# A fused two-block transformer kernel: memory keys interleaved with the mixing projection, and rotation by quarter-partition writes

## The chip, the cores and the metric

The kernel runs on one core of one Trainium2 chip. The metric is the device time of one launch in microseconds; lower is better. All matrix work here is float32, and TensorE (PE in the rows) is kept supplied by ScalarE (ACT), VectorE (DVE) and one DMA queue whose instructions SyncE (SPq) issues. GpSimd does next to nothing.

## The reference, cut to what matters

The reference is a transformer block with latent attention, memory cross-attention and a 16-expert layer, followed by a second block with gated linear attention. Only the first block holds the changed work:

```python
q_rope = apply_rope(q[..., QK_NOPE:], cos, sin)      # per head pair: 2 heads x 64 columns, 512 tokens
k_rope = apply_rope(kr, cos, sin)
y_mla  = mla_attention(q_nope, q_rope, k_nope, k_rope, v) @ w_mla_out
x = x + (g_conv * y_conv + g_mla * y_mla) @ w_mix_out            # the mixing projection
q = rmsnorm(x, norm_mem_g) @ w_mem_q                             # the memory norm feeds only q
k, v = split(rmsnorm(mem, norm_memkv_g) @ w_mem_kv)              # 256 memory rows, no need of x
# apply_rope: v1, v2 = halves of 32; out = [v1*cos - v2*sin, v1*sin + v2*cos]
```

Sizes: model width 1024 (8 tiles of 128), 512 tokens, 256 memory rows, 8 attention heads taken in 4 pairs, rotary width 64.

## The kernel before, in words

Activations lie transposed: model columns on the 128 partitions, tokens along the row. Every large product is made from three passes of float32r matmuls: each operand is split into a rounded high part and the rest, and `mm3` (L636 to L638) issues high by high, low by high and high by low. So a weight has to go through a small pipeline before TensorE may use it:

- SyncE loads a **unit** of 8 x 256 columns (1 MB) into one of two `raw` slots, once the unit two before it has been split (`w_lo_ready`).
- ScalarE makes the high part (`split_hi`, L1606), once TensorE has finished the unit two before it, whose slot it overwrites.
- VectorE makes the low part (`split_lo`, through `rest`, L2156), and TensorE may begin.

The order of units is the list `STREAM`, and all engines walk it in their own hand-written program order; each engine is strictly in order, and semaphores join them. A unit gives two output tiles of 128 columns. `dense_tiles` walks them with 24 matmuls each and cycles through four PSUM banks (`tile`), waiting until the earlier result in the bank has been consumed.

**The memory stage.** Four units of the mixing projection (`mix_out`, 512 tokens wide) come first; VectorE adds each result to `X`. Then come four units of memory keys (`mk`) and four of memory values (`mv`), each 256 columns wide, and after them four units of memory queries (`mq`), whose right-hand side is the normalised `X` in `H_hi` and `H_lo`. Their results of keys and values are split again by ScalarE (L1787) and VectorE (`mk_lo`, `mv_lo`). The norm of `X` runs inside the key and value units: squares (L1618), their sums, a matmul with ones (`norm_sums`, after `mk` unit 1), the root, a reciprocal (L2176), and then eight tiles, each made by VectorE into `T` (L2179), rounded by ScalarE (`his`, L1628) and its rest taken by VectorE (`h_lo`). `T` has two buffers. Which tiles follow which unit is the table `MEM_NORM_AT`. On ScalarE a unit is: copy of tile 0, `split_hi(u + 2)`, copy of tile 1, `his`. On VectorE it is: `split_lo(u + 2)`, the two rests, `norm_split`. The first tile of `mq` waits for `h_lo_ready` in front of each of its eight k steps, one norm tile more at each.

**The rotation.** For each head pair t the 128 rotary query rows `("qrope", t)` come out of TensorE. ScalarE copies them to `qr`; TensorE multiplies by a signed permutation `rot_c` (`rotate`, L741); VectorE (`rope`, L2282 to L2286) forms PSUM * sin + qr * cos, casts and takes the rest. Inside the pair loop the PE order behind the last transposes of a pair is `project_key(t+1, 0)`, `rotate`, `values(t, 3)`, `project_head(t+1, 1)`, then a wait for `queries(t+1, 0)` (`qk_lo_ready` 4t+5), `project_key(t+1, 1)`, a wait for `keys(t+1, 0)` (4t+6), two `project_value`, two `fill` and the scores of the next pair. VectorE runs `turned(t, 3)`, `queries`, `keys`, `rotated`. The same happens once to the keys' rotary rows `kr` (L708), in the first convolution unit.

**The experts** follow: their weights are streamed by SyncE into buffers that come free as TensorE finishes with them.

Of the kernel before, what the change touches and what calls it, by code (L numbers as in the profile page):

```python
# [63 lines left out]
for _name, _n in VEC_SIZES:  # L64
# [5 lines left out]
N_ROPE = 4  # L70
# [3 lines left out]
STREAM = [("lat", 2), ("conv", 12), ("conv_out", 4), ("glog", 8), ("mla_out", 4), ("mix_out", 4),  # L74
          ("memkv", 8), ("memq", 4), ("mem_out", 4), ("zk", 1), ("zlr", 1),
# [7 lines left out]

EUNITS = 12
MEM_NORM_AT = {2: (0, 1), 3: (2,), 4: (3, 4), 5: (5,), 6: (6, 7)}
# [69 lines left out]
def build(nc, t, out):  # L155
    with ExitStack() as ctx:
# [24 lines left out]
        rot_at = at[0]  # L181
        rot_c = fixed("rot_c", [P, P])
        tri = place("tri", [P, P], F32, rot_at)
# [56 lines left out]
        qr = place("qr", [P, S], F32, R + 113 * K)  # L240
# [141 lines left out]
        meta_sq_ready = sem("meta_sq_ready")  # L382
        meta_std_ready = sem("meta_std_ready")
        meta_n_ready = sem("meta_n_ready")
        meta_hi_ready = sem("meta_hi_ready")
        meta_lo_ready = sem("meta_lo_ready")
# [17 lines left out]
        qr_copied = sem("qr_copied")  # L404
# [208 lines left out]
        def _(pe):  # L613
# [60 lines left out]
            pe.wait_ge(meta_sq_ready, 1)  # L674
# [18 lines left out]
            for i in range(4):  # L693
                u = U0["conv"] + 3 * i
                dense_tiles(u, "xc", 2 * i, S, H, lambda m: (xc_copied, m + 1), ready=(h_lo_ready, 0))
                if i == 0:

                    pe.wait_ge(std_ready, 1)
                    pe.wait_ge(lat_sq_ready, 2)
                    for k in range(2):  # L700
                        ins = pe.matmul(bank[4][:, :], ones[:, :], sq[:, k, :], start=(k == 0), stop=(k == 1))
                    mark(ins, "ss_q")
                    pe.wait_ge(lat_sq_ready, 3)
                    pe.wait_ge(meta_std_ready, 1)
# [33 lines left out]
            def rotate(t, b):  # L738
                pe.wait_ge(qr_copied, t + 1)
                marks.tile = b  # L740
                mark(pe.matmul(b[:, :], rot_c[:, :], qr[:, :], start=True, stop=True), ("rot_q", t))  # L741

# [8 lines left out]
            for i in range(4):  # L751
                if i == 3:
# [4 lines left out]
                    rotate(0, bank[7])  # L757
                    w = unit(U0["conv_out"] + 3)
                    for j in range(2):
                        if j == 1:  # L760
                            project_head(0, 1, bank[4])
# [5 lines left out]
                            project_value(0, 1, bank[7])  # L767
# [73 lines left out]
            for t in range(PAIRS):  # L841
# [54 lines left out]
            for i in range(4):  # L896
                dense_tiles(U0["mix_out"] + i, "mix_out", 2 * i, S, H, lambda m: (x_ready, m + 1),
                            ready=(m_lo_ready, 0))

            M = [MM_hi, MM_lo]  # L900
            for i in range(4):
                dense_tiles(U0["memkv"] + i, "mk", 2 * i, MEM, M, lambda m: (mkv_ready, m + 1),
                            ready=(mem_lo_ready, 0))
                if i == 1:
                    norm_sums("mem")

            for i in range(4):
                u = U0["memkv"] + 4 + i
# [7 lines left out]
                marks.at[("unit", u)] = marks.at[("mv", i, 1)]  # L916
            for i in range(4):
# [680 lines left out]
        def _(act):  # L1598
# [32 lines left out]
            act.activation(meta_sq[:, :, :], meta[:, :, :], ACT.Square).then_inc(meta_sq_ready, 1)  # L1631
            for m in range(KT):
# [9 lines left out]
                if m == 2:  # L1642
                    done(act, "meta_ss")
                    act.activation(meta_sq[:, 0, :], bank[5][:, 0:META], ACT.Sqrt, bias=eps, scale=1.0 / D)\
                       .then_inc(meta_std_ready, 1)
# [6 lines left out]
            act.wait_ge(meta_n_ready, 1)  # L1652
            act.activation(meta_hi[:, :, :], meta[:, :, :], ACT.Copy).then_inc(meta_hi_ready, 1)
# [32 lines left out]
            for i in range(4):  # L1686
                if i == 3:
                    copy(("qrope", 0), qr[:, :], qr_copied)
# [28 lines left out]
            for t in range(PAIRS):  # L1717
# [15 lines left out]
                if more:  # L1733
                    copy(("qrope", t + 1), qr[:, :], qr_copied)
                    copy(("q", t + 1, 0), qn_hi[:, 0, :], qk_hi_ready)
# [35 lines left out]
            for i in range(4):  # L1771
                for k in (2 * i, 2 * i + 1):
                    act.wait_ge(mem_n_ready, k + 1)
                    act.activation(MM_hi[:, k, :], memx[:, k, :], ACT.Copy).then_inc(mem_hi_ready, 1)
                split_hi(U0["mix_out"] + i + 2)
            squares("mem")
            for i in range(8):
                for j in range(2):
                    if i < 4:
                        o = done(act, ("mk", 2 * i + j))  # L1780
                        dst = mk_hi[:, 2 * i + j, :]
                    else:
                        o = done(act, ("mv", i - 4, j))
                        dst = mv_hi[:, j, (i - 4) * UC:(i - 3) * UC]
                    if j:
                        split_hi(U0["memkv"] + i + 2)
                    act.activation(dst, o[:, 0:UC], ACT.Copy).then_inc(mkv_hi_ready, 1)  # L1787
                if i == 1:
                    root("mem")
                if i in MEM_NORM_AT:  # L1790
                    his("mem", MEM_NORM_AT[i])
# [124 lines left out]
            act.wait_ge(meta_lo_ready, 1)  # L1916
# [228 lines left out]
        def _(dve):  # L2145
# [72 lines left out]
            def latent(m, dst):  # L2218
# [8 lines left out]
            dve.wait_ge(meta_std_ready, 1)  # L2227
# [6 lines left out]
               .then_inc(meta_n_ready, 1)  # L2234
            dve.wait_ge(meta_hi_ready, 1)
            rest(meta_lo[:, :, :], meta[:, :, :], meta_hi[:, :, :]).then_inc(meta_lo_ready, 1)
# [43 lines left out]
            def rope(src, dst, o, s, hi, lo):  # L2280

                link(dve.tensor_tensor(out=T[:, 0, :], in0=o[:, :], in1=sin_t[:, :], op=ALU.mult))  # L2282
                link(dve.tensor_tensor(out=T[:, 1, :], in0=src, in1=cos_t[:, :], op=ALU.mult))
                link(dve.tensor_tensor(out=dst, in0=T[:, 0, :], in1=T[:, 1, :], op=ALU.add))
                link(dve.tensor_copy(hi, dst))
                rest(lo, dst, hi).then_inc(s, 1)  # L2286

            done(dve, "rot_k")
            dve.wait_ge(c_lo_ready, KT)
            dve.wait_ge(rope_in, 16 * N_ROPE)  # L2290
            rope(kr[:, :], kr[:, :], bank[6], lat_ready, kr_hi[:, :], kr_lo[:, :])
# [18 lines left out]
            def rotated(t):  # L2310
                o = done(dve, ("rot_q", t))
                rope(qr[:, :], qr[:, :], o, qrr_ready, qr_hi[:, :], qr_lo[:, :])

            for i in range(4):
                if i == 3:
                    queries(0, 0)
                    keys(0, 0)
                    rotated(0)
# [37 lines left out]
            for t in range(PAIRS):  # L2356
# [47 lines left out]
            for i in range(4):  # L2404
                for k in (2 * i, 2 * i + 1):
                    dve.wait_ge(mem_hi_ready, k + 1)
                    rest(MM_lo[:, k, :], memx[:, k, :], MM_hi[:, k, :]).then_inc(mem_lo_ready, 1)
                for m in (2 * i, 2 * i + 1):
                    o = done(dve, ("mix_out", m))
                    dve.tensor_tensor(out=X[:, m, :], in0=o[:, :], in1=X[:, m, :], op=ALU.add).then_inc(x_ready, 1)  # L2410
                split_lo(U0["mix_out"] + i + 2)
            accumulate("mem")
            dve.wait_ge(x_ready, KT)
            for i in range(8):
                split_lo(U0["memkv"] + i + 2)
# [854 lines left out]
```

## Time and profile before

| | |
|---|---|
| device time, three runs | 1876.14, 1876.35, 1881.18 us; median 1876.35 us |
| span of the profiled execution (first to last instruction) | 1877.1 us |
| the profiled execution's own time | not listed apart from the three runs |
| busy: PE, PE weight loads, DVE, ACT | 1831.2, 1365.5, 1007.7, 631.1 us |
| mean granted TensorE clock | 0.993 |
| HBM traffic | 321.25 MB read, 172 GB/s over the span |

A row of a timeline reads: start us, duration us, engine, line, operation, output <- inputs, shapes, count of merged instructions, and in brackets how long the engine had been idle before and what ended that. Back-to-back instructions overlap a little, so the distance between starts is what one of them costs its engine. Granted clock 1.00 is 2.4 GHz, 0.50 is 1.2 GHz.

### The profile page before, as it was taken

How to read it: one execution, taken by the hardware profiler on the slowest of the kernel's cores; microseconds unless marked ns; L12 is line 12 of the kernel's file. 1: busy time of each engine (PE TensorE's matmuls, PEld its weight loads, DVE VectorE, ACT ScalarE, POOL GpSimd, SP SyncE). 2: the span in 40 equal slices, each digit the busy share in tenths (PEclk: the TensorE clock that was granted, in tenths of full speed). 3: DMA queues.
4: the chain of work that ended last, by engine and by line, in shares of the span. 5: the costliest groups of instructions: out<-in, count | busy, mean ns of one | idle time of the engine just before them, and what ended most of it. 6: DMA issues, size and time to landing. Idle time of an engine off the chain costs nothing.

```text
span 1877.1 us, 23248 instructions
## 1 busy us (share of the span) xinstructions
PE 1831.2 (98%) x9860; PEld 1365.5 (73%) x9860; DVE 1007.7 (54%) x1472; ACT 631.1 (34%) x921; POOL 0.2 (0%) x4
## 2 busy tenths in 40 slices
PE   7999999999999999999999999999999999999998
PEld 6788777788887886343443443797888779988998
DVE  6654366633565643222212322756766799777775
ACT  5322245433243421211112111444442345343331
POOL 0000000000000000000000000000000000000000
PEclk9999999999999999999999999999999999999999
DMA  6223211032244327999999999323221223323231
GB/s 188 90 90 94 86 51 37 24 116 90 90 135 135 109 116 314 428 427 427 429 427 427 427 428 417 116 75 90 83 74 46 90 68 113 112 91 110 92 113 46
DMA packets 136007, 324.85 MB, mean 173 GB/s; under 512 B 7504, under 2 KB 118368, under 8 KB 122464
## 3 DMA queue, kind: packets, MB, share of 16 engines
q1 hardware_dynamic: 135760, 322.32, 46.2%
q8 instruction: 78, 1.28, 0.3%
q10 hardware_dynamic: 144, 1.05, 0.1%
q14 instruction: 25, 0.20, 0.0%
HBM read 321.25 MB, written 2.10 MB: 172 GB/s over the span
## 4 chain that ended last, share of the span: by engine, by line
PE 83%; DMA 8%; DVE 5%; ACT 2%; issue 1%; SPq 0%; DVEq 0%; ACTq 0%
PE bank L636 20%; PE bank L637 19%; PE bank L638 19%; PE bank L1124 12%; DMA ew_b<-in_w_exp_up 2%; DMA ew_f<-in_w_exp_up 2%; DMA ew_g<-in_w_exp_up 2%; DMA ew_c<-in_w_exp_up 2%; PE bank L1148 2%; PE bank L835 2%; PE bank L1083 1%; PE bank L1324 1%; DVE w_lo L2156 1%; ACT w_hi L1606 1%; DMA raw<-in_w_in 1%
## 5 line engine op out<-in xcount | busy, mean ns | idle before, releaser
L636 PE MATMUL bank<-H_hi,w_hi 128*128 128x512 f32 (+2 forms) x992 | 375.8, 379 | 3.4 <-DVE H_lo L2156 1.8
L637 PE MATMUL bank<-H_lo,w_hi 128*128 128x512 f32 (+2 forms) x992 | 371.0, 374 | 0.0
L638 PE MATMUL bank<-H_hi,w_lo 128*128 128x512 f32 (+2 forms) x992 | 370.9, 374 | 0.0
L2156 DVE TENSOR_TENSOR w_lo<-raw,w_hi 128x2048 fp32r<-128x2048 f32 (+2 forms) x110 | 209.8, 1920 | 186.0 <-ACT w_hi L1606 173.0
L636 PEld LDWEIGHTS bank<-H_hi,w_hi 128*128 128x128 f32 x992 | 186.9, 188 | 47.2 <-issue 8.4
L638 PEld LDWEIGHTS bank<-H_hi,w_lo 128*128 128x128 f32 x992 | 186.9, 188 | 36.1
L637 PEld LDWEIGHTS bank<-H_lo,w_hi 128*128 128x128 f32 x992 | 186.9, 188 | 35.1 <-issue 0.7
L1606 ACT ACTIVATE w_hi<-raw 128x2048 fp32r<-128x2048 f32 x74 | 141.2, 1908 | 128.0 <-PE bank L638 120.4
L2568 DVE SCALAR_TENSOR_TENSOR SG<-bank,gs,SG 128x512 f32<-128x512 f32 x16 | 11.3, 746 | 206.6 <-PE bank L1124 206.6
L636 PE MATMUL bank<-C_hi,w_hi 128*128 128x512 f32 x160 | 65.9, 412 | 4.8 <-DVE C_lo L2209 4.7
L638 PE MATMUL bank<-C_hi,w_lo 128*128 128x512 f32 x160 | 64.6, 404 | 0.0
L637 PE MATMUL bank<-C_lo,w_hi 128*128 128x512 f32 x160 | 64.5, 403 | 0.0
L1897 ACT ACTIVATE AT<-bank 128x512 f32<-128x512 f32 x16 | 9.6, 598 | 146.8 <-PE bank L1135 146.7
L2086 ACT ACTIVATE p<-bank 128x256 f32<-128x256 f32 x42 | 16.2, 385 | 124.9 <-PE bank L638 124.9
L2156 DVE TENSOR_TENSOR chunk_lo<-TK,chunk_hi 128x512 fp32r<-128x512 f32 x56 | 35.6, 688 | 41.9 <-ACT chunk_hi L1861 41.6
L1124 PE MATMUL bank<-ew_b,XG 128*64 128x512 f32 x224 | 51.1, 610 | 2.7 <-DMA ew_b<-in_w_exp_up 2.7
L1124 PE MATMUL bank<-ew_c,XG 128*64 128x512 f32 x224 | 49.5, 594 | 2.1 <-DMA ew_c<-in_w_exp_up 2.1
L638 PE MATMUL bank<-FF_hi,w_lo 128*128 128x512 f32 x128 | 50.6, 395 | 0.0
L637 PE MATMUL bank<-FF_lo,w_hi 128*128 128x512 f32 x128 | 50.6, 395 | 0.0
L636 PE MATMUL bank<-FF_hi,w_hi 128*128 128x512 f32 x128 | 50.6, 395 | 0.0
L1124 PE MATMUL bank<-ew_d,XG 128*64 128x512 f32 x96 | 43.7, 609 | 3.0 <-DMA ew_g<-in_w_exp_up 3.0
L1124 PE MATMUL bank<-raw,XG 128*64 128x512 f32 x96 | 42.3, 593 | 2.7 <-DMA ew_f<-in_w_exp_up 2.7
(586 smaller groups left out, 3877.9 us busy)
## 6 DMA issues: line engine op xcount, KB each, us to landing
raw<-in_w_in SPq DMA_DIRECT2D x36, 1024.0 KB, 5.5
raw<-in_w_ff SPq DMA_DIRECT2D x32, 1024.0 KB, 5.5
ew_b<-in_w_exp_up SPq DMA_DIRECT2D x8, 2048.0 KB, 27.4
ew_c<-in_w_exp_gate SPq DMA_DIRECT2D x8, 2048.0 KB, 27.0
ew_c<-in_w_exp_up SPq DMA_DIRECT2D x6, 2048.0 KB, 30.6
ew_b<-in_w_exp_gate SPq DMA_DIRECT2D x6, 2048.0 KB, 23.9
raw<-in_w_mem_kv SPq DMA_DIRECT2D x8, 1024.0 KB, 5.4
ew_d<-in_w_exp_up SPq DMA_DIRECT2D x4, 2048.0 KB, 26.1
```

The costliest lines, as they stand in the source:

```text
L636: pe.matmul(o, lhs[0], rhs[0], start=first, stop=False, **kw)
L637: pe.matmul(o, lhs[0], rhs[1], start=False, stop=False, **kw)
L638: return pe.matmul(o, lhs[1], rhs[0], start=False, stop=last, **kw)
L835: ins = pe.matmul(bank[7][:, c:c + P], vt[:, h, j, :], pt[:, h, j, :], start=(j == 0), stop=(j == TT - 1))
L1083: ins = pe.matmul(bank[4 + half][:, :], OH[:, tt, :], part[c % 3][:, :], start=(tt == 0 and part is chunk_hi), stop=(tt == TT - 1 and part ...
L1124: ins = pe.matmul(acc[half][r, :], lhs[:, k, r], views[e][:, j, half * S:(half + 1) * S], start=(k == 0), stop=(k == KT - 1))
L1148: ins = pe.matmul(o[:, :], part[:, m * P:(m + 1) * P], OT[:, p % 2, :], start=(part is YO_hi), stop=(part is YO_lo))
L1324: ins = pe.matmul(o[:, i * P:(i + 1) * P], a[r, hp, o0 + cp * P:o0 + (cp + 1) * P], b[r, hp, cp * P:(cp + 1) * P], start=True, stop=True)
L1606: act.activation(w_slot(u, True), raw[:, u % RAW, :], ACT.Copy).then_inc(w_hi_ready, 1)
L2086: act.activation(dst, o[:, 0:HS], ACT.Copy).then_inc(part_copied, 1)
L2156: return dve.tensor_tensor(out=dst, in0=src, in1=hi_part.bitcast(F32), op=ALU.subtract)
L2568: dve.scalar_tensor_tensor(out=SG[:, c], in0=up_banks(p)[half][:, :], scalar=gs[:, p % 2, 1:2], in1=SG[:, c], op0=ALU.mult, op1=ALU.mult). ...
```

## The change

Two edits and some bookkeeping.

1. The mixing units and the key units form one list `MIXED` in `STREAM`, and the loads follow it. All eight `MM_hi` / `MM_lo` splits of the memory rows move in front of it. The norm's squares and sums follow the mixing units 2 and 3, `norm_sums` comes after `mk` unit 2, and the norm tiles are placed one unit later in the weight order than before.
2. The permutation matmul, its constant, the copy `qr` and their semaphores go. `sin` carries the sign. VectorE writes four products of 32 partitions each into `T`, each to the other half of its 64 rows. In the pair loop and before it `rotated` moves in front of `keys`, and in the loop in front of `queries` too. `project_head(., 1)` takes a bank of its own.
3. Five semaphores for the meta tokens become two, with the same order of events; `tri` takes the place of `rot_c` in memory.

```diff
+MIXED = [("mix", 0), ("mix", 1), ("mk", 0), ("mix", 2), ("mk", 1), ("mix", 3), ("mk", 2), ("mk", 3),
+         ("mv", 0), ("mv", 1), ("mv", 2), ("mv", 3)]
-MEM_NORM_AT = {2: (0, 1), 3: (2,), 4: (3, 4), 5: (5,), 6: (6, 7)}
+MEM_NORM_AT = {("mk", 3): (0, 1), ("mv", 0): (2,), ("mv", 1): (3, 4), ("mv", 2): (5,), ("mv", 3): (6, 7)}
...
-                    pe.wait_ge(lat_copied, 4)
-                    pe.wait_ge(rope_in, 16 * N_ROPE)
-                    mark(pe.matmul(bank[6][:, :], rot_c[:, :], kr[:, :], start=True, stop=True), "rot_k")
...
-                    pe.wait_ge(exp_done, 8 * t + 8)
-                    rotate(t + 1, bank[4])
                 values(t, 3)
                 if more:
-                    project_head(t + 1, 1, bank[1])
+                    pe.wait_ge(exp_done, 8 * t + 8)
+                    project_head(t + 1, 1, bank[4])
...
+            for n, (kind, i) in enumerate(MIXED):
+                u = U0["mixed"] + n
+                if kind == "mix":
+                    dense_tiles(u, "mix_out", 2 * i, S, H, lambda m: (x_ready, m + 1), ready=(m_lo_ready, 0))
+                elif kind == "mk":
+                    dense_tiles(u, "mk", 2 * i, MEM, M, lambda m: (mkv_ready, m + 1), ready=(mem_lo_ready, 0))
+                    if i == 2:
+                        norm_sums("mem")
+                else:
+                    values_unit(u, i)
...
+            def rope(src, s, hi, lo):
+
+                half = ROPE // 2
+                for b in range(0, P, half):
+                    dst = b ^ half
+                    dve.tensor_tensor(out=T[dst:dst + half, 0, :], in0=src[b:b + half, :], in1=sin_t[b:b + half, :], op=ALU.mult)
+                link(dve.tensor_tensor(out=T[:, 1, :], in0=src[:, :], in1=cos_t[:, :], op=ALU.mult))
+                link(dve.tensor_tensor(out=T[:, 0, :], in0=T[:, 0, :], in1=T[:, 1, :], op=ALU.add))
+                link(dve.tensor_copy(hi, T[:, 0, :]))
+                rest(lo, T[:, 0, :], hi).then_inc(s, 1)
...
                 turned(t, 3)
                 if more:
+                    rotated(t + 1)
                     queries(t + 1, 0)
                     keys(t + 1, 0)
-                    rotated(t + 1)
```

`link` makes VectorE wait for the instruction it has just issued.

## Rows read from the trace of the kernel before

**Rows 1.** The page's part 1: busy time, share of the span, instructions.

```profile
PE 1831.2 (98%) x9860; PEld 1365.5 (73%) x9860; DVE 1007.7 (54%) x1472; ACT 631.1 (34%) x921; POOL 0.2 (0%) x4
```

**Rows 2.** Waits of PE between 525 and 640 us: total, times, longest.

```profile
PE bank L636 <- DVE mv_lo L2156: 3.0, 2, 2.5
...
PE bank L636 <- DVE mk_lo L2156: 0.7, 1, 0.7
```

**Rows 3.** Windows: stretch, length, busy PE PEld DVE ACT POOL, clock, DMA.

```profile
525.60:577.70 52.10, 47.95 (x389) 45.97 (x388) 38.68 (x42) 27.67 (x37) 0.00 (x0) 1.00 0.44 142
480.80:525.60 44.80, 44.80 (x193) 36.03 (x192) 24.11 (x32) 10.84 (x13) 0.00 (x0) 1.00 0.30 95
```

**Rows 4.** Timeline of DVE, memory stage: splits of units mv1 to mq1, last norm tiles.

```profile
553.75 2.29 DVE L2156 TENSOR_TENSOR w_lo<-raw,w_hi 128x2048 fp32r<-128x2048 f32 x1 [1.38 <-ACT w_hi L1606]
...
560.14 2.29 DVE L2156 TENSOR_TENSOR w_lo<-raw,w_hi 128x2048 fp32r<-128x2048 f32 x1 [2.77 <-ACT w_hi L1606]
...
568.59 2.29 DVE L2156 TENSOR_TENSOR w_lo<-raw,w_hi 128x2048 fp32r<-128x2048 f32 x1 [2.77 <-ACT w_hi L1606]
...
574.98 2.29 DVE L2156 TENSOR_TENSOR w_lo<-raw,w_hi 128x2048 fp32r<-128x2048 f32 x1 [1.38 <-ACT w_hi L1606]
...
579.30 1.35 DVE L2156 TENSOR_TENSOR H_lo<-T,H_hi 128x512 fp32r<-128x512 f32 x2
582.04 2.29 DVE L2156 TENSOR_TENSOR w_lo<-raw,w_hi 128x2048 fp32r<-128x2048 f32 x1 [1.38 <-ACT w_hi L1606]
```

**Rows 5.** Timeline of ACT: the split that waits for PE, not for the norm.

```profile
544.67 1.92 ACT L1606 ACTIVATE w_hi<-raw 128x2048 fp32r<-128x2048 f32 x1 [2.50 <-PE bank L638]
```

**Rows 6.** Chain of work in time: PE's first matmul of the memory queries.

```profile
577.71 0.47 PE bank L636
```

**Rows 7.** Timeline of DVE at the end of the second head pair.

```profile
305.11 0.69 DVE L2341 COPY pt<-bank 128x512 f32<-128x512 f32 x1 [3.60 <-PE bank L822]
305.72 0.68 DVE L2156 TENSOR_TENSOR qn_lo<-bank,qn_hi 128x512 fp32r<-128x512 f32 x1
...
307.21 0.68 DVE L2282 TENSOR_TENSOR T<-bank,sin_t 128x512 f32<-128x512 f32 x1
307.93 0.69 DVE L2283 TENSOR_TENSOR T<-qr,cos_t 128x512 f32<-128x512 f32 x1
308.65 0.69 DVE L2284 TENSOR_TENSOR qr<-T 128x512 f32<-128x512 f32 x1
309.38 0.43 DVE L2285 CAST qr_hi<-qr 128x512 fp32r<-128x512 f32 x1
309.84 0.69 DVE L2156 TENSOR_TENSOR qr_lo<-qr,qr_hi 128x512 fp32r<-128x512 f32 x1
310.45 0.68 DVE L2156 TENSOR_TENSOR C_lo<-bank,C_hi 128x512 fp32r<-128x512 f32 x1
```

**Rows 8.** Timeline of PE in the same stretch.

```profile
305.77 1.02 PE L741 MATMUL bank<-qr,rot_c 128*128 128x512 f32 x2
306.63 1.95 PE L835 MATMUL bank<-pt,vt 128*128 128x128 f32 x16
...
309.82 1.02 PE L736 MATMUL bank<-ckvn,ukv_w 128*128 128x512 f32 x2
310.67 1.95 PE L746 MATMUL bank<-ukv_w,ckvn 128*128 128x128 f32 x16
...
315.25 0.40 PE L636 MATMUL bank<-kn_hi,qn_hi 128*128 128x512 f32 x1
```

**Rows 9.** DVE group by form: a two-input instruction on 16 partitions.

```profile
L2627 DVE TENSOR_TENSOR lrt<-bank,s_tok 16x264 f32<-16x264 f32 x2 | 0.7, 409 | 0.0
```

**Rows 10.** Windows around three idle stretches of PE.

```profile
568.00:571.40 3.40, 0.87 (x9) 0.70 (x7) 2.81 (x3) 0.82 (x2) 0.00 (x0) 1.00 0.00 0
...
1030.80:1034.20 3.40, 0.69 (x6) 0.16 (x4) 0.00 (x0) 0.00 (x0) 0.00 (x0) 0.99 1.01 429
1034.20:1037.60 3.40, 3.40 (x10) 1.16 (x11) 0.00 (x0) 0.00 (x0) 0.00 (x0) 0.50 1.00 424
```

**Rows 11.** Timeline of the DMA queue: first of the loads that keep it full.

```profile
710.11 0.80 SPq L3139 DMA_DIRECT2D ew_c<-in_w_exp_up x2
```

More of the change, by code:

```diff
@@ L895, in _, with values_unit @@
                     mark(ins, "mem_ss")
-            for i in range(4):
-                dense_tiles(U0["mix_out"] + i, "mix_out", 2 * i, S, H, lambda m: (x_ready, m + 1),
-                            ready=(m_lo_ready, 0))
             M = [MM_hi, MM_lo]
[L901 to L908, printed above, removed]
+            def values_unit(u, i):
                 w = unit(u)
@@ L1770, in _ @@
                        .then_inc(mem_std_ready, 1)
[L1771 to L1777, printed above, removed]
+            for k in range(KT):
+                act.wait_ge(mem_n_ready, k + 1)
+                act.activation(MM_hi[:, k, :], memx[:, k, :], ACT.Copy).then_inc(mem_hi_ready, 1)
+            for n, (kind, i) in enumerate(MIXED):
+                u = U0["mixed"] + n
+                if kind == "mix":
+                    split_hi(u + 2)
+                    if i == 2:
+                        squares("mem", range(6))
+                    elif i == 3:
+                        squares("mem", (6, 7))
+                    continue
                 for j in range(2):
-                    if i < 4:
+                    if kind == "mk":
                         o = done(act, ("mk", 2 * i + j))
@@ L2316, in _ @@
                     queries(0, 0)
+                    rotated(0)
                     keys(0, 0)
-                    rotated(0)
                     queries(0, 1)
@@ L2412, in _ @@
[L2412 to L2415, printed above, removed]
+            for k in range(KT):
+                dve.wait_ge(mem_hi_ready, k + 1)
+                rest(MM_lo[:, k, :], memx[:, k, :], MM_hi[:, k, :]).then_inc(mem_lo_ready, 1)
+            for n, (kind, i) in enumerate(MIXED):
+                u = U0["mixed"] + n
+                if kind == "mix":
+                    for m in (2 * i, 2 * i + 1):
+                        o = done(dve, ("mix_out", m))
+                        dve.tensor_tensor(out=X[:, m, :], in0=o[:, :], in1=X[:, m, :], op=ALU.add).then_inc(x_ready, 1)
+                    split_lo(u + 2)
+                    if i == 2:
+                        accumulate("mem", range(1, 5))
+                    elif i == 3:
+                        accumulate("mem", range(5, KT - 1))
+                        dve.wait_ge(x_ready, KT)
+                    continue
+                split_lo(u + 2)
@@ L3122, in _ @@
             matrix("mla_out", t["w_mla_out"], 4)
-            matrix("mix_out", t["w_mix_out"], 4)
-            matrix("memkv", t["w_mem_kv"], 8)
+            for n, (kind, i) in enumerate(MIXED):
+                w, c0 = (t["w_mix_out"], 0) if kind == "mix" else (t["w_mem_kv"], D if kind == "mv" else 0)
+                load(U0["mixed"] + n, columns(w, c0 + i * UC))
             matrix("memq", t["w_mem_q"], 4)
@@ L3212, in constants @@
     half = ROPE // 2
-    rot = np.zeros((P, P), np.float32)
-    for b in range(0, P, ROPE):
-        for i in range(half):
-            rot[b + half + i, b + i] = -1.0
-            rot[b + i, b + half + i] = 1.0
-    c["rot"] = rot
     c["tri"] = np.triu(np.ones((P, P), np.float32))
```

101 lines of the change are left out of this document (36 added, 65 removed).

## Prediction

> **What bounds the kernel now.** I read the page first: PE is busy 98% of the span [rows 1], so a change gains only where it removes PE work or one of PE's few waits, and it loses wherever it makes a new one. Next the waits of PE around the memory stage: it waits for `mv_lo` 3.0 us and for `mk_lo` 0.7 us [rows 2]. The windows put a price on the stretch: the mixing units fill PE completely, 44.8 us for four of them, 11.2 each; the eight key and value units and the norm's sums take 52.1 us with PE busy for 47.95, so about 4.2 us stand idle there [rows 3]. That is all that an interleaving can win in this stage.
>
> What ends those waits is a ring between two engines. The split of a weight unit by VectorE waits for ScalarE's half, ScalarE stands behind `his`, which stands behind the `T` tiles, which VectorE makes only after the last split and its rests. The starts of five splits show it: 553.75, 560.14, 568.59, 574.98, 582.04 [rows 4], distances of 6.39 (one norm tile, number 2), 8.45 (tiles 3 and 4), 6.39 (tile 5) and 7.06 (tiles 6 and 7; tiles 0 and 1 run through the same chain and I give them 7.06 too). A unit of 256 columns costs PE half of a mixing unit, 5.6 us. Every one of these turns is longer than that. The mean lead of the ring is eaten up at the end, and PE starts the memory queries at 577.71 [rows 6], 2.73 us behind the start of the split at 574.98 [rows 4].
>
> **The interleaving, step by step.** I walk the new order from PE's start of mixing unit 0 at 480.8 [rows 3]. Units 0 to 7 of the new list are four wide and four narrow ones: 4 x 11.2 + 4 x 5.6 = 67.2. A wide unit follows or precedes each of the first key units, so a split that starts some 0.3 us after PE's end of a unit and lasts 1.9 on ScalarE [rows 5] and 2.3 on VectorE [rows 4], 4.4 in all, lies under the 5.6 of the shorter neighbour: no wait. The norm's sums after `mk` 2 are two float32 matmuls of 512 columns; one costs 0.86 (305.77 to 306.63 in [rows 8]), so 1.7, and with the wait for the last sum of squares and the turn-round I take 2.3. PE ends `mk` 3 at 480.8 + 67.2 + 2.3 = 550.3.
>
> From here on the order is `mk` 3, then four value units with nothing wide between them, and all eight norm tiles lie behind these last five. ScalarE's half of `mv` 1 can start at 550.6, VectorE's at 552.5. Before, it was 553.75 [rows 4]: the ring starts 1.25 us earlier. It then turns as before, with one unit less behind it: split of `mv` 2 at 552.5 + 7.06 = 559.6, of `mv` 3 at + 6.39 = 565.95, of query unit 0 at + 8.45 = 574.4, of query unit 1 at + 6.39 = 580.8. PE starts `mq` 0 at 574.4 + 2.73 = 577.1, which is 0.6 earlier than before.
>
> But tiles 6 and 7 now come after the split of query unit 1, where before they came after that of unit 0. Before, the split at 574.98 was followed by the two `H_lo` at 579.30 for 1.35 [rows 4]: the first ended 5.0 us behind the split's start, the second 5.7. Now they end at 580.8 + 5.0 = 585.8 and 586.5. The first `mq` tile needs tile 6 at its seventh k step, 6/8 of 5.6 = 4.2 us after 577.1, at 581.3. PE waits 4.5 us with everything else queued behind it. The tile ends at 586.5 + 0.7 + 0.1 = 587.3 instead of 577.7 + 5.6 = 583.3: **+4.0 us**. What is late next is the copy of that tile by ScalarE, and all of it moves with PE. The early split of the memory rows (eight rests in front of the list) ends some 8 us before the first key unit, and the additions to `X` are taken at the same distance from PE as before; both cost nothing, and if the cover were gone it would be the 1.3 us of two extra pairs of rests. The loads keep their sizes and distances, since each is issued at a split.
>
> **The rotation.** Removed: five permutation matmuls of 0.86 us (305.77 to 306.63 in [rows 8]). The one for the keys and the one for pair 0 stand in full PE work: 2 x 0.86 = **-1.7 us**. There VectorE's longer rotation lies under convolution output units of 11.2 us, which want a split only every 11.2, so it costs nothing; uncovered it would be 2.2 each.
>
> In the pair loop the same matmul goes three times, but `rotated` now stands in front of `queries`. Take the end of the second pair. VectorE copies `pt` at 305.11 and was free for `queries` at 305.72 [rows 7]. Now four quarter products come first. A dependent product costs 0.72 (307.21 to 307.93), independent ones of that shape 0.61 (305.11 to 305.72) [rows 7]. A product of 16 partitions and 264 columns takes 409 ns [rows 9], more than half of the 680 of 512 columns and 128 partitions [rows 7], so the time goes by columns, and a quarter of the partitions costs a whole instruction. No row has neighbours on different quarters; between 0.61 and 0.72 I take the slower. The rotation is 4 x 0.72 + 0.72 + 0.73 (308.65 to 309.38) + 0.46 + 0.61 (309.84 to 310.45) [rows 7] = 5.4, so `queries` starts at 311.1 and ends at 311.8, and `keys` ends at 312.4. PE, without the permutation, starts `values` at 305.85 instead of 306.63 and ends `project_head` 3.19 later (306.63 to 309.82 in [rows 8]), at 309.04. Then it waits for `queries`: 2.8 us, up to 311.85. From its next product (309.82) to the scores (315.25) it takes 5.43 as before [rows 8], so the scores start at 317.3, not 315.25: +2.04 us. Behind the wait stand `project_key`, both `project_value` and two `fill`, all of which could have run. Three times: **+6.1 us**. With 0.61 it is 1.6 each, +4.8.
>
 By that rule the quarters would follow at the dependent distance, which gives the sum below; without it the sum would be 1.3 us less.
>
> **The clock.** A PE idle of 3.3 us (busy 0.69 of 3.4) was followed by 3.4 us at 0.50, that is 1.2 GHz, and one of 2.8 around 568 by none [rows 10]. Such a fall costs half of 3.4 us, 1.7, where PE has work. The 4.5 us wait in `mq` 0 should bring one, part of it inside the wait: 0 to 1.7, I take 0.9. Of the three waits of 2.8 us I take one: 1.7, with bounds 0 and 5.1. **+2.6 us**.
>
> **Does it reach the end?** The DMA queue is full through the experts, share 1.01 [rows 10], but the stream begins with an issue at 710.11 [rows 11] that waits for PE. A delay in front of it moves the stream and the end alike. The semaphores' merging and the smaller constants change no order: 0, and no row excludes some tenths either way.
>
> **Sum.** 4.0 - 1.7 + 6.1 + 2.6 = 11.0 us. The profiled span is 1877.1 and the median of the runs 1876.35, 0.04% apart; the sum is put on the median: **1887.4 us**. Bounds of the parts: quarters at 0.61 and no fall of the clock give 4.0 - 1.7 + 4.8 = 7.1; a fall at each wait gives 4.0 - 1.7 + 6.1 + 6.8 = 15.2. So the likeliest case has 1883 to 1892.
>
> **Rivals.** (A) *A quarter costs a quarter.* Four products then cost as much as one; the rotation is 3.24, `queries` ends at 309.6, PE waits 0.65, and each pair gains 0.2: 4.0 - 1.7 - 0.6 + 0.9 = +2.6, 1879. Against it stands the row by columns [rows 9]. (B) *The other side: the ring no longer binds.* If ScalarE and VectorE turned in 5.6 us or less, PE would start `mq` at 480.8 + 89.6 + 2.3 = 572.7, 5.0 us earlier, with tiles 6 and 7 in time. It decides when `H_lo` 6 is there 4.2 us after `mq` starts; by my walk it comes 8.7 after. Then -5.0 - 1.7 + 6.1 + 1.7 = +1.1, 1877.5, no change. For it speaks that the squares and sums leave the narrow units; against it that each turn in the trace is over 6.3 with norm tiles [rows 4]. (C) *The clock takes more*: every wait brings a fall, and one more behind; over 1891. (D) *The delay is absorbed* in the experts because some of their weights are loaded ahead; 1876 to 1880. Against it stands the late start of the stream [rows 11].
>
> **How the numbers follow.** Likeliest case 0.66, A 0.08, B 0.10, C 0.08, D 0.08. A measurement of this kernel tells about 0.3%, 5.6 us, from no change. Slower by more than that is over 1882.0: the likeliest case and C, 0.74. A, B and D are within it but for a small part: same 0.20. Faster would need a gain of 5.6 us, more than all of the idle in the stage: 0.06, for a trace that shows less than I think. The range runs from 1878, which takes in A, to 1892, which takes in all of the likeliest case; B, most of D and half of C lie outside, some 0.2.
>
> **What the profile of the changed kernel would show.** Right: PE waits for `qn_lo` three times, 2.4 to 2.8 us; quarter products 0.61 to 0.72 apart, each near 680 ns; PE waits once some 4.5 us for `H_lo` in the first query tile, and about 3 us for `mv_lo`; no PE wait between the first key units; half-clock stretches right behind the long waits. Wrong: quarter products under 0.3 us; no `qn_lo` wait; memory queries starting near 573; the expert stage ending at the same time although the memory stage ended later. The prediction is most open in the clock, and in the ring, where a turn 0.5 us shorter would take 2 us off the wait.

## The result, and the profile after

The changed kernel took 1896.46 us (median of four runs, 1895.96 to 1896.98) against 1878.76 for the kernel before in the same comparison: ratio 1.0087, 95% interval 1.0066 to 1.0108. It is slower, 17.7 us in the medians, where 11.0 had been forecast. A second comparison gave 1894.1 against 1880.66: 1.0069, interval 1.0042 to 1.0096. Both kernels spread far more than I had thought: the kernel before ran from 1874.4 to 1886.2 over the runs of all comparisons, the changed one from 1888.4 to 1899.8.

The page of the changed kernel, the row that answers to [rows 1]:

```profile
PE 1836.6 (97%) x9850; PEld 1369.0 (72%) x9850; DVE 1018.3 (54%) x1487; ACT 629.5 (33%) x917; POOL 0.2 (0%) x4
```

TensorE runs ten instructions fewer (the five permutation products, two instructions each) and is busy 5.4 us longer. Fewer instructions cannot do that; a lower clock can.

The waits of PE in the changed kernel, first from 230 to 400 us and then from 525 to 640, to be read beside [rows 2]:

```profile
PE bank L728 <- DVE qn_lo L2147: 8.3, 3, 2.8
...
PE bank L631 <- DVE H_lo L2147: 2.8, 1, 2.8
PE bank L631 <- DVE w_lo L2147: 2.5, 1, 2.5
PE bank L631 <- DVE mv_lo L2147: 1.1, 2, 0.6
PE bank L660 <- DVE sq L2161: 0.3, 1, 0.3
```

In the kernel before, the only wait of PE between 240 and 385 us was this one:

```profile
PE bank L835 <- ACT pt L1681: 0.2, 1, 0.2
```

So the pair loop, which had no wait for VectorE, now has three of 2.8 us. VectorE at the end of the second pair shows why; this answers to [rows 7]:

```profile
306.19 0.69 DVE L2333 COPY pt<-bank 128x512 f32<-128x512 f32 x1 [3.59 <-PE bank L808]
306.92 2.79 DVE L2276 TENSOR_TENSOR T<-bank,sin_t 32x512 f32<-32x512 f32 x4
309.72 0.69 DVE L2277 TENSOR_TENSOR T<-bank,cos_t 128x512 f32<-128x512 f32 x1
310.44 0.69 DVE L2278 TENSOR_TENSOR T<-T 128x512 f32<-128x512 f32 x1
311.17 0.43 DVE L2279 CAST qr_hi<-T 128x512 fp32r<-128x512 f32 x1
311.63 0.69 DVE L2147 TENSOR_TENSOR qr_lo<-T,qr_hi 128x512 fp32r<-128x512 f32 x1
312.24 0.68 DVE L2147 TENSOR_TENSOR qn_lo<-bank,qn_hi 128x512 fp32r<-128x512 f32 x1
```

and TensorE in the same stretch, to be read beside [rows 8]:

```profile
309.80 0.40 PE L633 MATMUL bank<-cqn_hi,uq_lo 128*128 128x512 f32 x1
312.98 1.77 PE L728 MATMUL bank<-ckvn,ukv_w 128*128 128x512 f32 x2 [2.78 <-DVE qn_lo L2147]
314.54 3.01 PE L733 MATMUL bank<-ukv_w,ckvn 128*128 128x128 f32 x16
...
320.17 0.39 PE L631 MATMUL bank<-kn_hi,qn_hi 128*128 128x512 f32 x1
```

From the product at 312.98 to the scores (the first products of the next pair's queries with its keys) at 320.17 it takes 7.19 us, where the same instructions took 5.43 [rows 8]. Behind the wait the clock is at half, and that costs 1.76. The windows around the waits at the end of the second and the third pair:

```profile
309.60:313.00 3.40, 0.62 (x4) 0.18 (x2) 3.28 (x7) 0.60 (x1) 0.00 (x0) 1.00 0.00 0
313.00:316.40 3.40, 3.40 (x11) 2.47 (x12) 2.41 (x4) 0.60 (x1) 0.00 (x0) 0.55 0.00 0
353.90:357.40 3.50, 0.72 (x3) 0.28 (x3) 3.40 (x6) 0.60 (x1) 0.00 (x0) 1.00 0.00 0
357.40:360.80 3.40, 3.40 (x13) 2.64 (x13) 2.15 (x4) 0.99 (x2) 0.00 (x0) 0.54 0.02 5
```

The memory stage of the changed kernel, VectorE, to be read beside [rows 4] (the splits belong to the same units, `mv` 1 to `mq` 1):

```profile
561.40 2.29 DVE L2147 TENSOR_TENSOR w_lo<-raw,w_hi 128x2048 fp32r<-128x2048 f32 x1 [1.63 <-ACT w_hi L1593]
...
568.45 2.29 DVE L2147 TENSOR_TENSOR w_lo<-raw,w_hi 128x2048 fp32r<-128x2048 f32 x1 [1.38 <-ACT w_hi L1593]
...
574.85 2.29 DVE L2147 TENSOR_TENSOR w_lo<-raw,w_hi 128x2048 fp32r<-128x2048 f32 x1 [2.77 <-ACT w_hi L1593]
...
583.30 2.29 DVE L2147 TENSOR_TENSOR w_lo<-raw,w_hi 128x2048 fp32r<-128x2048 f32 x1 [2.78 <-ACT w_hi L1593]
...
589.69 2.29 DVE L2147 TENSOR_TENSOR w_lo<-raw,w_hi 128x2048 fp32r<-128x2048 f32 x1 [1.38 <-ACT w_hi L1593]
...
594.01 1.36 DVE L2147 TENSOR_TENSOR H_lo<-T,H_hi 128x512 fp32r<-128x512 f32 x2
```

and TensorE's first query tile, which answers to [rows 6]:

```profile
586.03 0.47 PE L631 MATMUL bank<-H_hi,w_hi 128*128 128x512 f32 x1 [2.50 <-DVE w_lo L2147]
...
591.61 0.39 PE L633 MATMUL bank<-H_hi,w_lo 128*128 128x512 f32 x1
594.75 0.50 PE L631 MATMUL bank<-H_hi,w_hi 128*128 128x512 f32 x1 [2.75 <-DVE H_lo L2147]
```

The distances of the splits are 7.05, 6.40, 8.45 and 6.39, as before; the tile starts 2.73 behind its split, and its seventh k step stands still until `H_lo` 6 is there, 5.0 us behind the last split's start. The wait of 2.5 us in front of the tile was followed by half clock, from 586.4 to 589.8, under its first k steps.

When both traces are laid side by side and the same TensorE instruction is looked up in each, the changed kernel stands as follows against the one before: -2.0 us at the end of pair 0; +1.0, +4.9, +8.8 at the first scores of pairs 1, 2, 3; +8.85 at the first mixing product; +12.9 at the second memory query tile and up to 700 us; +12.1 at 1170; +13.6 at 1240; +18.3 at 1450, and +18.2 at 1600. The last step is made in a stage that no edit touches, the products of the four heads in the second block ("the heads" from here on). Window of the changed kernel there, and of the kernel before in the same work:

```profile
1453.40:1463.60 10.20, 10.20 (x38) 8.87 (x38) 1.50 (x2) 1.19 (x2) 0.00 (x0) 0.50 0.00 0
```

```profile
1437.80:1441.30 3.50, 3.50 (x30) 3.19 (x28) 0.51 (x2) 0.60 (x1) 0.00 (x0) 1.00 0.02 8
```

10.2 us at half clock with PE busy for all of them, against none. Between 1440 and 1466 us it moves the products behind it by 4.7 us, of the 18.2, and it was not in my sum. The "late stretch" below is this one. Before a cause could be named it had to be told whether the edits bring this stretch or chance does.

### The profile page after: what moved, and what is told of

It reads as the page before. It is cut to its first block, busy times and chain, and to the rows that moved or that the text cites. A ratio compares the mean times of both kernels' runs of the same rounds, so it can differ in the third digit from the quotient of the medians.

```text
span 1895.1 us, 23234 instructions
## 1 busy us (share of the span) xinstructions
PE 1836.6 (97%) x9850; PEld 1369.0 (72%) x9850; DVE 1018.3 (54%) x1487; ACT 629.5 (33%) x917; POOL 0.2 (0%) x4
## 4 chain that ended last, share of the span: by engine, by line
PE 83%; DVE 7%; DMA 6%; ACT 2%; issue 1%; SPq 0%; DVEq 0%; ACTq 0%
PE bank L631 19%; PE bank L633 19%; PE bank L632 19%; PE bank L1111 13%; DMA ew_f<-in_w_exp_up 2%; DMA ew_b<-in_w_exp_up 2%; DMA ew_g<-in_w_exp_up 2%; PE bank L1135 2%; PE bank L821 1%; PE bank L1070 1%; ACT w_hi L1593 1%; PE bank L1311 1%; DVE w_lo L2147 1%; PE bank L798 1%; PE bank L808 1%
## 5 line engine op out<-in xcount | busy, mean ns | idle before, releaser
L2565 DVE SCALAR_TENSOR_TENSOR SG<-bank,gs,SG 128x512 f32<-128x512 f32 x16 | 11.3, 747 | 208.4 <-PE bank L1111 208.4
```

## The experiments

In the tables "full-clock span" is a run's span times its mean granted clock, and "lost to the clock" is the rest of the span; both are medians over the runs. The clock is listed to 0.001, 1.9 us of a single run, so the two columns are good to about 1 us.

### The changed kernel again

> The changed kernel again, beside the others, for the spread of its runs. Theory L (local waits and the half clock at them) says 8.5 us of waits, less 2 for the removed products, plus 1.7 to 5 of clock: 10 to 12 above the kernel before. Theory C says that the 18 us of its first comparison hold 5 to 8 us of clock that falls in stages no edit touches, different from run to run: a spread of 5 to 10 us, and a median between 10 and 18 above. Rival (a fixed loss in a later stage): every run again 18 above.

Measured: 1894.1 us, runs 1888.38, 1888.91, 1889.45, 1898.75, 1899.01, 1899.80. The kernel before, 29 runs: 1880.66, from 1875.07 to 1886.18, eight of them within 1875.1 to 1875.7 at clock 0.995 or 0.996. So both kernels have a bottom group of runs, and runs well above it (an upper group). Bottom against bottom it is 1888.9 to 1875.4, +13.5 us; the upper three of the changed kernel lie 10 us above its lower three. The rival of a fixed loss is out: 18 above is not what every run gives.

### One part alone

`e_rot` is the kernel before with the rotation part of the diff, `e_mem` the kernel before with `MIXED` and all that follows it.

> The rotation part alone on the kernel before; memory stage as before. Theory L (only the waits at the edited places and the half-clock stretches right behind them): in the trace -2.0 us up to the end of pair 0, three waits for qn_lo of 2.8, +2.15 each, 1.7 for each wait that is followed by half clock, so +4.5 with none and +9.6 with three. Theory C (the clock also falls at other places in stages that no edit touches, and where it falls depends on the whole timing): the total differs from the trace's shift behind the pairs by some multiple of 1.7 us, either way, up to 7. Rival: the rotation is cheap and the loss is in the memory stage, total within 1 us.

Measured: 1885.87 against 1878.25, ratio 1.0040, interval 1.0022 to 1.0057. In the trace -3.3 us at the end of pair 0 (2.6 for three removed products, the rest mostly from the start-up, which varies), +8.9 at the first scores of pair 3, and 9.0 at 700 us; half clock behind all three waits, for which +9.6 had been expected.

> The interleaving alone on the kernel before; rotation with the permutation matmul. Theory L: +4.0 us, all between mixing unit 0 and the end of the first memory query tile, by the wait for H_lo 6 and 7 at the seventh k step. Theory C: the same +4.0 in the trace there, and the total off from it by a multiple of 1.7. Rival (the interleaving gains the idle it was aimed at): -4 to -5.

Measured: 1884.5 against 1878.25, ratio 1.0031, interval 1.0014 to 1.0048; the fastest run 1878.47, 4.0 above the 1874.42 of the kernel before. In the trace the stretch from the first mixing product to the second memory query tile is 112.19 us, where the kernel before has 108.17: the 4.0 that was expected. The waits of PE in `e_mem` there:

```profile
PE bank L638 <- DVE H_lo L2166: 2.7, 1, 2.7
PE bank L638 <- DVE w_lo L2166: 2.5, 1, 2.5
```

Each part loses by itself, and the interleaving gains nothing of the idle that it was aimed at.

### Undoing one position each

`e_order` is the changed kernel with this edit, and the same in front of the pair loop:

```diff
                 if more:
-                    rotated(t + 1)
                     queries(t + 1, 0)
                     keys(t + 1, 0)
+                    rotated(t + 1)
```

> The changed kernel with rotated moved back behind queries and keys. Theory L: the three waits for qn_lo go (PE finds queries done 3 us before it asks) and with them the half clock behind two of them: the scores of the next pair start 3.0 (2.15 + 0.86) earlier in each pair, less at most 0.3 if the chain through the quarter products reaches the scores first; 9 to 12 us faster than the changed kernel, so 1885 to 1888. Rival (quarters are the cost wherever they stand): the wait moves to the scores and is as long, no gain.

Measured: 1883.73 us, runs 1874.88 to 1888.05, against 1878.25: ratio 1.0021, interval 1.0002 to 1.0040. That is 10.4 and 12.7 below the two medians of the changed kernel, and below the 1885 to 1888 that I had expected. VectorE at the end of the second pair in `e_order`:

```profile
301.95 0.68 DVE L2147 TENSOR_TENSOR qn_lo<-bank,qn_hi 128x512 fp32r<-128x512 f32 x1
302.83 0.69 DVE L2147 TENSOR_TENSOR kn_lo<-bank,kn_hi 128x512 fp32r<-128x512 f32 x1 [0.20 <-ACT kn_hi L1668]
303.55 2.79 DVE L2276 TENSOR_TENSOR T<-bank,sin_t 32x512 f32<-32x512 f32 x4
```

The quarter products cost the same 2.79, but PE has no wait for `qn_lo` in the whole loop, and each pair is 0.6 to 0.7 us shorter than in the kernel before instead of 2.2 to 3.9 longer. The rival that the wait moves to the scores is out: at most 0.2 to 0.3 of the removed 0.86 is given back there. The memory stage keeps the wait for `H_lo`, and in this profile the clock fell behind both of its long waits (573.7 and 580.5): +5.3 us there, not 4.0.

`e_norm` is the changed kernel with the norm tiles taken two by two:

```diff
-MEM_NORM_AT = {("mk", 3): (0, 1), ("mv", 0): (2,), ("mv", 1): (3, 4), ("mv", 2): (5,), ("mv", 3): (6, 7)}
+MEM_NORM_AT = {("mk", 3): (0, 1), ("mv", 0): (2, 3), ("mv", 1): (4, 5), ("mv", 2): (6, 7)}
```

> The changed kernel with norm tiles (0,1), (2,3), (4,5), (6,7) behind mk 3, mv 0, mv 1, mv 2, so that none comes behind mv 3. Theory L: turns of 7.06 three times, 0.7 less in all than before; H_lo 6 and 7 are there in time; PE starts the first query tile 0.7 us earlier and runs through it: 5.3 us less than the changed kernel's memory stage, 1.3 less than the one of before. Theory C: the same in the trace, the total off by multiples of 1.7. Rival (the ring is not what bounds): the wait is seen at another buffer and the stage costs the same.

Measured: 1890.25 us, 1882.57 to 1893.60. In the trace the stage goes from +9.07 at the first mixing product to +7.87 at the second query tile, 1.2 less than in the kernel before, where 1.3 was expected, and 5.2 less than in the changed kernel, where 5.3 was. The waits of PE from 230 to 640 us in `e_norm`:

```profile
PE bank L728 <- DVE qn_lo L2147: 8.3, 3, 2.8
PE bank L631 <- DVE mv_lo L2147: 1.8, 2, 1.1
...
PE bank L631 <- DVE w_lo L2147: 1.1, 1, 1.1
```

The wait for `H_lo` is gone; 2.9 us for the ring remain.

### Both positions undone

> The changed kernel with both repairs: rotated behind keys, and norm tiles by pairs behind mk 3, mv 0, mv 1, mv 2. Theory L: up to the memory stage 4 to 5 us ahead of the kernel before (as the trace of the run with rotated moved back shows), and 1.2 more in the memory stage: 5 to 6 us faster than before, about 1872 where before has 1878. Theory C: that, with the spread of the clock on it, 2 to 8. Rival: the removed products were free cover and nothing is gained, 0.

Measured: 1870.82 us (1869.65 to 1880.17) against 1880.66, ratio 0.9959, interval 0.9942 to 0.9976. Repeated as `e_both2`:

> The version with both repairs again, beside the next one: 1870 to 1872, 8 to 10 us below the kernel before, with single runs 5 to 7 us higher, those in which the clock falls for 10 to 14 us at 1434 to 1455 in the head products of the second block.

Measured: 1877.02 us (1869.84 to 1878.39) against 1880.13, ratio 0.9970, interval 0.9953 to 0.9987. I had expected 1870 to 1872 with single runs above, and that median missed: seven of the twelve lay above. The two medians differ by 6 us because the runs of one and the same kernel have two groups, around 1870.4 and from 1875 to 1880: 7 and 5 of twelve in the first comparison, 5 and 7 in the second. Bottom against bottom it is 5.0 us faster than the kernel before, 1870.4 to 1875.4. This version beats both kernels.

### A pure delay

`d_5` and `d_10` put a delay into the kernel before and change nothing else:

```diff
             pe.wait_ge(exp_done, 8 * PAIRS)
+            for _ in range(5):        # d_10: range(10)
+                pe.matmul(bank[5][:, :], ones[:, :], sq[:, 0, :], start=True, stop=True)
             n_tile[0] = 1
```

> The kernel before with five extra float32 products of 512 columns (0.86 us each) on TensorE behind the pair loop, a pure delay of 4.3 us before everything that follows; nothing else changes, the output neither. Theory L: +4.3, no more. Theory C in its simple form (falls by chance, as often as before): +4.3 in the median, with the same spread. Theory P (where the clock falls is fixed by the time at which a stage is reached): the total jumps by other than 4.3, by several us, and the runs lie together.

> The same with ten extra products, a pure delay of 8.6 us, as long as the shift that the rotation edit makes. Theory L and C: +8.6 in the median. Theory P: off by several us from that, and not by the same amount as with five. In the trace a half-clock stretch of 10 us or more around 1440 to 1450 (seen in the changed kernel, not in the one before) would show that a delay alone can bring it.

Measured: 1882.71 and 1885.78 against 1880.66, so +2.1 and +5.1 in the medians; the middles of the bottom groups are 1879.7 and 1884.2, +4.3 and +8.8 on 1875.4, which is the delay itself. Upper groups lie some 7 us above the bottoms. So a delay moves the kernel by its own length, and over the runs no more is lost to the clock than without it (12.2 and 11.3 against 13.2 in the table); the medians are moved by how many runs happen to fall into the upper group. Theory P is out. Neither profiled run has a long late stretch, so these two don't show that a delay alone brings one.

They do show half clock coming and going at one and the same wait. PE waits 2.5 us for `mv_lo` in the memory stage of the kernel before (568.8 to 571.4), and so it does in `e_rot`, `d_5` and `d_10`, whose memory stage is the same. The clock stayed up behind it in the first two and fell for 3.4 us in the two delayed ones (at 574.7 and 579.7), and that made their stage 0.8 and 0.9 us longer.

| kernel | median us | lowest | full-clock span | lost to the clock |
|---|---|---|---|---|
| before (29 runs) | 1880.66 | 1875.07 | 1864.4 | 13.2 |
| changed, first comparison | 1896.46 | 1895.96 | 1871.0 | 23.7 |
| changed, second comparison | 1894.10 | 1888.38 | 1872.5 | 18.9 |
| `e_rot` | 1885.87 | 1884.14 | 1869.0 | 15.1 |
| `e_mem` | 1884.50 | 1878.47 | 1867.7 | 15.1 |
| `e_order` | 1883.73 | 1874.88 | 1864.5 | 17.9 |
| `e_norm` | 1890.25 | 1882.57 | 1868.8 | 18.9 |
| `e_both` | 1870.82 | 1869.65 | 1859.7 | 9.3 |
| `e_both2` | 1877.02 | 1869.84 | 1859.7 | 14.1 |
| `d_5` | 1882.71 | 1878.84 | 1868.5 | 12.2 |
| `d_10` | 1885.78 | 1884.02 | 1873.7 | 11.3 |
| `e_warm` (below) | 1892.06 | 1886.06 | 1873.6 | 17.0 |
| `e_heads` (below) | 1879.45 | 1876.68 | 1866.8 | 11.3 |

### Keeping TensorE at work in the new waits

`e_warm` is the changed kernel with this in the pair loop, and four such products (`bank[7]`, `sq`) in front of k step 6 of the first query tile:

```diff
                     project_head(t + 1, 1, bank[4])
+                    for _ in range(3):
+                        pe.matmul(bank[6][:, :], ones[:, :], ckvn[:, :], start=True, stop=True)
                     pe.wait_ge(qk_lo_ready, 4 * t + 5)
```

> The changed kernel with TensorE kept at work in its new waits: three extra float32 products (2.6 us) in front of each wait for queries in the pair loop, four (3.4 us) in front of the seventh k step of the first memory query tile; their results are not used. If the half clock behind the waits (268 to 272, 313, 357, 586) comes from TensorE standing idle: the places keep their local delay, but the half-clock stretches there are gone and the time is 3 to 6 us below the changed kernel's 1894. Rival (the clock falls at these moments for another reason): same stretches, same time.

Measured: 1892.06 us, 1886.06 to 1892.43, where the changed kernel had 1888.38 to 1899.80. Its windows at the three waits:

```profile
266.00:269.40 3.40, 3.19 (x9) 1.34 (x8) 3.30 (x6) 0.60 (x1) 0.00 (x0) 1.00 0.00 0
309.60:313.00 3.40, 3.19 (x11) 1.40 (x10) 3.33 (x7) 0.15 (x1) 0.00 (x0) 1.00 0.00 0
353.90:357.40 3.50, 3.29 (x21) 2.65 (x21) 2.73 (x5) 1.45 (x3) 0.00 (x0) 1.00 0.00 0
```

No half clock follows any of them up to 581 us. The traces with idle waits have it behind three waits (`e_rot`, `e_norm`) or two (the changed kernel, both profiles). So it is the idling that brings it there, as far as one profile with three filled waits can show. From the scores of one pair to those of the next it is 42.5 us three times, where the changed kernel has 42.5, 44.2 and 44.1: a fall of the clock behind such a wait costs 1.6 to 1.7 us. The gain in time of the whole, 2.0 in the medians and 2.3 between the fastest runs, is below the 3 to 6 expected, and six runs don't separate it from chance. The half-clock stretch of the memory stage stayed, at 581 us, behind the wait for the weight split, which this kernel does not fill.

### The late stretch

> The version with both repairs, and in the second block two extra full-size float32 products (1.7 us) in front of the small ones of each of the four heads, 6.9 us in all; results not used. Theory H (the late half-clock stretch of 10 to 14 us comes because these products of 64 rows and 64 columns use little of the array though TensorE counts as busy): no stretch there in the trace, the runs lie together, median at 1877 to 1878, and the slowest run gains on the slowest of the version without. Rival (chance, whatever runs there): 6.9 us slower in all runs with the same two clusters.

```diff
                     o = tile((og_n_ready, OGN[f"s{h}"]))
+                    for _ in range(2):
+                        pe.matmul(o[:, :], ones[:, :], v2[:, 0, :], start=True, stop=True)
                     for cp in range(TT):
```

Measured: 1879.45 us, 1876.68 to 1882.29, against `e_both2` in the same comparison with 1877.02, 1869.84 to 1878.39. The same work in `e_both2` and in `e_heads`:

```profile
1432.80:1436.20 3.40, 3.40 (x23) 3.29 (x24) 0.66 (x1) 0.60 (x1) 0.00 (x0) 0.74 0.00 0
1436.20:1439.60 3.40, 3.40 (x17) 3.18 (x16) 0.09 (x1) 0.00 (x0) 0.00 (x0) 0.50 0.00 0
```

```profile
1433.40:1436.80 3.40, 3.40 (x19) 2.32 (x19) 0.33 (x2) 0.42 (x2) 0.00 (x0) 1.00 0.00 0
1436.80:1440.20 3.40, 3.40 (x19) 2.38 (x19) 0.75 (x1) 0.60 (x1) 0.00 (x0) 1.00 0.00 0
```

The spread shrinks from 8.6 to 5.6 us, the lowest run rises by the 6.9 of the extra products (1869.8 to 1876.7), the highest by 3.9 only. By the rival all runs should have risen by 6.9 and kept their two groups. So the late stretch makes most of the upper group, and a remainder of some 3 us has another source. It is no repair: the cover costs what it saves.

### Reading all profiles for the late stretch

Thirteen profiles were at hand. Seven have the late stretch (the changed kernel twice, `e_mem`, `e_norm`, `e_both`, `e_both2`, `e_warm`) and six don't (the kernel before, `e_rot`, `e_order`, `d_5`, `d_10`, `e_heads`). All seven hold the interleaved memory stage, and that looks like a cause; but `e_order` holds it too and has none, and `e_heads` has it with the heads covered. The length of the stretch, and how far the profiled run lay above the lowest run of its kernel:

| profiled run above the kernel's lowest, us | profile, and length of its late stretch |
|---|---|
| 0.0, 1.0, 1.3, 2.1, about 3, 4.3 | `e_rot`, `d_5`, `d_10`, `e_heads`, before, `e_order`: none |
| 5.7, 6.6, 8.0, 8.5, 10.6 | `e_warm`, `e_mem`, `e_both2`, changed, changed again: 10.2 us |
| 10.3, 10.5 | `e_norm`, `e_both`: 13.7 us |

(The kernel before has no listed time for its profiled run; "about 3" comes from its span. The changed kernel is set against its lowest run, 1888.38.) The stretch moves the products behind it by 4.7 us where it is 10.2 long and by some 6.2 where it is 13.7, and the profiles with it are the slow ones of their kernels, without an exception. So the late stretch is most of what parts the upper runs from the lower. What decides whether a run has it is not shown. All profiles without it are of low runs, so they can't tell whether the upper runs of `d_5`, `d_10` and the kernel before, which lie 7 to 12 us above the lowest, have it too.

## Why the prediction was wrong

**Direction and mechanisms were right.** Slower, by waits for `qn_lo` and for `H_lo` 6, at the places named.

**The ring.** Distances forecast 7.06, 6.39, 8.45, 6.39, measured 7.05, 6.40, 8.45, 6.39. The loss of the stage was put at 4.0 us and measured as 12.88 - 8.85 = 4.0. Only its shape is different: the wait in the tile is 2.8 us and not 4.5, because half clock had made the six k steps before it longer by the rest. A clock that falls in front of a wait is paid by the wait, so its 0.9 us in my sum was 0 in this profile and in `e_mem`. In the second profile of the changed kernel and in `e_order` the clock fell once more behind the wait for `H_lo` itself (at 594.8 and 580.5), and the stage was 5.5 and 5.3 us longer instead of 4.0. The sign "about 3 us for `mv_lo`" came as 1.1 for `mv_lo` and 2.5 for `w_lo`.

**The rotation.** The four quarters took 2.80 us from the first to the next product (306.92 to 309.72), 0.70 each, close to the slow one of my two bounds. By the Trainium skill, "VectorE: DVE Perf Modes", section "Two Vector instructions with no wait between them", they would be held apart; the trace agrees, with 0.70 where neighbours on the same partitions follow at 0.61 (311.63 to 312.24). The first quarter is held as well: it follows the copy of `pt` at 0.73 instead of 0.61. An instruction on 32 partitions takes 680 to 697 ns, as one on 128 does; rival A is out. The pair cost was forecast as 2.04 and measured, where the clock stayed up, as 2.15 (-1.12 at the scores of pair 0, +1.03 at those of pair 1). The -1.12 is the two removed products, 1.7, less some 0.35 that the start-up took longer in this run and 0.25 lost in front of the scores, which `e_order` does not lose. One reading was off without effect: `values` would start at 305.77 (306.63 - 0.86), not 305.85, and PE waits for VectorE either way.

**Local waits together.** 4.0 - 1.7 + 6.1 = 8.4 forecast; the full-clock spans differ by 1872.5 - 1864.4 = 8.1.

**The clock is the step that failed.** The forecast had 2.6 us. The table has 18.9 - 13.2 = 5.7 in the second comparison. The spans and clocks of the four runs in the first give 20.8, 24.6, 22.7 and 24.6 lost, a median of 23.7, 10.5 above 13.2. Two errors are in it.

First, of the three waits of 2.8 us I took one to bring half clock; it was two in both profiles of the changed kernel, and three in `e_rot` and `e_norm`. The rows had been misread: the idle stretches in [rows 10] are 2.71 us (3.40 - 0.69), which was followed by a fall, and 2.53 (3.40 - 0.87), which was not, where the prediction has 3.3 and 2.8. Read rightly, the new waits of 2.8 were longer than the one that had brought a fall, and three falls, 5.1 instead of 1.7, was the likelier term; with it the sum is 14.4. The stretch of 2.53 that had stayed without was no ground either: the same wait had a fall behind it in `d_5` and `d_10`.

Second and larger, I took the clock elsewhere as fixed. Rival C had "one more behind" and got 0.08, but the trace of one run can't show that the stretches in the unchanged stages come and go: the late one cost 4.7 us in the profiled run, another near 1231 some 1.5. That such losses need no edit is what the kernel before and the pure delays say: run by run the kernel before loses from some 9 us to the clock (0.995) to some 21 (0.989), and the delayed kernels have the same two groups. The fall near 1231 is in both profiles of the changed kernel and in none of the other eleven, and what brings it is open.

All four runs of the changed kernel in its first comparison lay in the upper group, two of the four of the kernel before did too, and so 17.7 us stood there for a difference of 13.5. Even that 13.5 is 2.5 more than the 11.0 of the sum, and the clock has it: with 8.1 for the local waits some 5.4 are left for half clock, where the sum had 8.4 and 2.6.

**What stays open.** The table of the late stretch rests on thirteen profiles and was made after they were there. What decides which run has the stretch is not known, and neither is whether the edits make it more frequent: seven of the ten runs of the changed kernel lie above its bottom group, and 49 of the 76 of the kernel before above its own (1874.4 to 1875.9), which is no difference. The forecast range ended at 1892 and its base was the median of three runs, two of them from the bottom; on the 1880.66 of the later runs the same sum gives 1891.7, which is still 2.4 below 1894.1.

**Rivals B and D.** B is out by the ring's distances. D as well: +12.9 at 700 us was still +12.1 at 1170. Both figures hold half clock of either profile (in between the shift went down to +9.0 and up again), so the pure delays are the better evidence: they stand in front of the experts, and the bottom groups end later by the whole 4.3 and 8.8.

## What to carry to other kernels

On an in-order engine, an instruction group that feeds nobody soon must stand behind the ones that another engine will ask for next: the same eight VectorE instructions of the rotation made a pair 2.2 to 3.9 us longer in front of `queries` and left it 0.6 shorter, by the removed product, behind `keys`. When work is interleaved to cover a norm, look for what the last norm tiles stand behind; their positions in one table were worth 5.2 us. And where half clock comes and goes between runs of one kernel, take the lowest group of many runs or span times clock, because a median of three can be off by more than the edit.

## What the runs showed of the hardware that was not expected

- The kernel before ran at 1875.1 to 1875.7 or at 1877.4 to 1886.2 in one and the same comparison, with mean clocks from 0.996 to 0.989. The Trainium skill, "TensorE: Matmul & The Clock Gate", Part 1, says that how many products run at the low clock differs from run to run of one kernel, and puts the penalty of that ramp at under 1% of a typical kernel span. The spread here, 12 us of 1880, is 0.6%: within that figure, and still as large as what the two edits cost together.
- The clock fell while TensorE counted as busy for the whole time: 10.2 us at 0.50 in the products of two heads (of 64 rows and 64 columns, and of 128 by 128) and the nine full-size ones behind them. It was there in seven profiles of thirteen, all of them of the slower runs of their kernel.
- One wait of 2.5 us in a stage that is the same in four kernels was followed by half clock in two profiles (`d_5`, `d_10`) and not in the two others (the kernel before, `e_rot`).
- Waits of 2.8 us were followed by half clock in 10 of the 12 cases that four profiles hold (the changed kernel twice, `e_rot`, `e_norm`), for 3.4 us each time. Filled with useless products the same waits were followed by none, in three.
